# Second attention: the bias table in three bf16 parts on two column halves, and the reached matrices made by VectorE

## The chip, the cores and the metric

The kernel runs on one core of one Trainium2 chip. The time is the device time of one execution in microseconds (us); 3 runs of the kernel before are given, and their median is the reference. Less is better.

## The reference, cut to what matters

The reference is two transformer blocks over 256 tokens of width 1024, in float32. The second block holds, beside a state space branch, a sparse attention, and only this one is touched. For each of 256 queries and 16 heads the logits over 256 keys are a product with a latent of 128 numbers, plus a bias that depends on the distance between key and query, plus a mask that leaves the 64 best keys:

```python
bias = rel_bias[t5_bucket_2(pos_sel - pos_b[..., None])]       # 32 buckets, 16 heads
logits = jnp.einsum('bqhc,bqkc->bhqk', q_b, kv_sel).astype(jnp.float32) * scale
logits = logits + jnp.transpose(bias, (0, 3, 1, 2)).astype(jnp.float32)
logits = jnp.where(valid[:, None], logits, -jnp.inf)
probs = jax.nn.softmax(logits, axis=-1).astype(kv_sel.dtype)
return jnp.einsum('bhqk,bqkc->bqhc', probs, kv_sel)
```

## The kernel before

Weights stream through a ring of four 128x1024 tiles. Each is split into a high part (ScalarE, line 826, written as fp32r) and a low part (VectorE at line 1229, or GpSimd at line 655), and TensorE multiplies three combinations of high and low parts; in most stages that is line 1772 (`fm_tile`, six matmuls for one row block k: two column blocks of 128 with three products each). Every engine runs its own list of instructions in the order in which they are written, and semaphores join them.

The second attention is worked off in 32 tiles of 8 queries x 16 heads = 128 rows (`NTILE`, `QT`). For tile n TensorE adds up in one PSUM bank `lg` of 128 rows x 256 keys:

- the product of queries and latent, `uq` and `kvT`, in fp32 (line 2192, one matmul that the trace shows as two instructions),
- the bias: the jumps of the bias from bucket to bucket are in a table, one row for each bucket border; `reached[c]` has a 1 where a key lies past the border. The 128 contraction rows are 32 borders x 4 queries, so the 8 queries of a tile take two such matrices, c = 0 and 1. The table of c is zero in the 64 columns of the other four queries. It exists as a high and a low fp32r part, `tab_hi` and `tab_lo`, so that line 2196 is four matmuls of 128 columns of weights and 256 moving columns,
- the mask, one bf16 matmul (line 2197, in the trace's numbering).

Then follow, in the same list, for older tiles: two transposes of the probabilities of tile n-2 (line 2205), for even n one step of `fm_tile` of another product (`s_z2`, line 1772) as filler, and the product of probabilities and values of tile n-3 (line 2216). Behind the 32 tiles stands the head-wise output product (line 2223).

GpSimd makes `reached` (line 760): two `tensor_scalar` for each tile, into two buffers; for tile n it waits until TensorE is through with the logits of tile n-2. TensorE waits for it with `reach_ready`.

VectorE does for tile n: the row maximum (line 1604, behind the logits of n), the reciprocal and the scaling of the probabilities of n-1 (lines 1609 and 1610), the copy of the output of n-4 (line 1615), and at n = 0, 8, 16, 24 the low parts of the filler's weights (`split_to`, line 1229). ScalarE does the exponential (line 1123) and the copy of the transposed probabilities (line 1130), and the high parts at the same n.

The table is made about 55 us earlier: VectorE multiplies it out into `tab_f` (line 1558, fp32), ScalarE makes `tab_hi` (line 1097), and VectorE the rest `tab_lo` behind the few instructions that prepare the step sizes of the state space branch (lines 1564 to 1569). Next on VectorE comes the sum of the index scores (lines 1580 and 1582).

Of the kernel before, what the change touches and what calls it, by code (L numbers as in the profile page):

```python
# [21 lines left out]
F32 = mybir.dt.float32  # L22
F32R = mybir.dt.float32r
BF16 = mybir.dt.bfloat16
I32 = mybir.dt.int32
ALU = mybir.AluOpType
ACT = mybir.ActivationFunctionType
AX = mybir.AxisListType

P = 128  # L30
S = 256
# [21 lines left out]
H2, CKV = 16, 128  # L53
# [3 lines left out]
QT = 8  # L57
NTILE = S // QT
# [57 lines left out]
def _emit(nc, ctx, a, out):  # L116
    def sem(name):
        return ctx.enter_context(nc.semaphore(name))

    def sb(name, shape, dt=F32, where=ctx):  # L120
        return where.enter_context(nc.sbuf_tensor(name, shape, dt))

    bank = [ctx.enter_context(nc.psum_tensor(f"bank{i}", [P, 512], F32)) for i in range(8)]
# [8 lines left out]
    sb("before_pick", [P, 2, S], F32, before_pick)  # L133
    pick = sb("pick", [P, 16 * P], BF16, before_pick)
    before_pick.close()
    ff_hi = sb("ff_hi", [P, KF, S], F32R)
    ff_lo = sb("ff_lo", [P, KF, S], F32R)
    x_tok = sb("x_tok", [P, TT, D])
    work = sb("work", [P, KD, S])
# [107 lines left out]
    kin = oT_flat[:, 1024:1280].rearrange("p (t a d) -> p t a d", t=TT, a=2)  # L247
    junk = oT_flat[:, 1280:1280 + 6 * QR].rearrange("p (n k) -> p n k", n=6)

    reached = ff_hi[:, 16:20, :].rearrange("p (b c) s -> p b c s", b=2)  # L250
    tab_hi, tab_lo = (ff_lo[:, 16 + i, :].rearrange("p (c m) -> p c m", c=2) for i in range(2))
    work_flat = work[:, :, :].rearrange("p k s -> p (k s)")
    sums2 = work_flat[:, 0:512].unsqueeze(1)
    p2T = work_flat[:, 512:1024].rearrange("p (b k r) -> p b k r", b=2, k=2)
# [119 lines left out]
    def held_slot(u):  # L374
# [61 lines left out]
    reach_ready, lt_mm, lt_max, lt_exp, lt_p, lt_T, lt_pT, lt_pv, lt_o = (  # L436
        sem("reach_ready"), sem("lt_mm"), sem("lt_max"), sem("lt_exp"), sem("lt_p"), sem("lt_T"),
        sem("lt_pT"), sem("lt_pv"), sem("lt_o"))
    step_mm, tab_own, tab_split = sem("step_mm"), sem("tab_own"), sem("tab_split")
    uv_mm, uv_hi, uv_lo = sem("uv_mm"), sem("uv_hi"), sem("uv_lo")  # L440

    dt_a, dt_b, dt_ready, xbc_ready = (
# [158 lines left out]
    def _(pool):  # L601
# [150 lines left out]
        pool.wait_ge(ix_sum, 8)  # L752
        pool.dma_start(w_uv[:, :, :], a["w_uv_2"].rearrange("h c d -> c h d")).then_inc(uv_in, 16)

        pool.wait_ge(tab_ready, 1)
        for n in range(NTILE):
            if n >= 2:
                pool.wait_ge(lt_mm, n - 1)
            for c in range(2):
                ins = pool.tensor_scalar(reached[:, n % 2, c, :], pos_f[:, 0:S],  # L760
                                         own_pos[:, 2 * n + c:2 * n + c + 1], None, ALU.is_ge)
            ins.then_inc(reach_ready, 1)
        pool.wait_ge(uv_mm, 4)
        for j in range(4):
            load_ada(8, j)
# [37 lines left out]
    def _(act):  # L803
# [233 lines left out]
        for n in range(len(TILES1) + 2):  # L1037
# [10 lines left out]
            if n >= 2:  # L1048
                m = n - 2
# [42 lines left out]
        for b in range(s_qi.n):  # L1092
            before_block(s_qi, b)
            act.activation(qi[:, 2 * b:2 * b + 2, :], bank3[(s_qi.b0 + b) % 2], ACT.Copy
                           ).then_inc(act_read, 1)
        act.wait_ge(tab_own, 1)
        act.activation(tab_hi, tab_f_cm, ACT.Copy).then_inc(tab_split, 1)

        for r in range(8):
            act.wait_ge(ix_mm, r + 1)  # L1100
# [118 lines left out]
    def _(dve):  # L1219
# [8 lines left out]
        def lo_of(dst, src, hi):  # L1228
            return dve.tensor_tensor(dst, src, hi.bitcast(F32), ALU.subtract)  # L1229
# [319 lines left out]
        for k in range(2):  # L1549
# [5 lines left out]
        lo_of(ff_lo[:, 0:2, :], rn[:, :, :], ff_hi[:, 0:2, :]).then_inc(qn_lo, 1)  # L1555
        split_to(s_qi.u0 + 4)
        dve.wait_ge(step_mm, 1)
        dve.tensor_tensor(tab_f[:, :, :], bank[6][:, 0:H2].unsqueeze(1).broadcast_to([P, 2 * QT, H2]),
                          own_query.unsqueeze(2).broadcast_to([P, 2 * QT, H2]), ALU.mult).then_inc(tab_own, 1)

        dve.wait_ge(few_T, 2)
        dve.wait_ge(ssd_in, 48)
# [4 lines left out]
        link(dve.scalar_tensor_tensor(dt_sc[:, 1, :, :], dt_sc[:, 0, :, :], -1.0, dt_sc[:, 0, :, :],  # L1567
                                      ALU.mult, ALU.max))
        dve.tensor_scalar(dt_sc[:, 0, :, :], dt_sc[:, 0, :, :], 0.0, None, ALU.max).then_inc(dt_a, 1)
        dve.wait_ge(tab_split, 1)  # L1570
        lo_of(tab_lo, tab_f_cm, tab_hi).then_inc(tab_ready, 1)

        for r in range(8):
            qt, r4 = r // 4, r % 4
# [21 lines left out]
        dve.tensor_tensor(mask[:, :, :], isc[:, :, :], shut[:, :, :], ALU.add).then_inc(mask_ready, 1)  # L1596
        split_to(s_z2.u0)

        for n in range(NTILE + 4):
            if n < NTILE:  # L1600
                dve.wait_ge(lt_mm, n + 1)
                if n >= 4:
                    dve.wait_ge(lt_exp, n - 3)
                dve.tensor_reduce(st3[:, n % 4, 0:1], bank[2 + n % 2][:, 0:S], AX.X, ALU.max, negate=True
                                  ).then_inc(lt_max, 1)
            if 1 <= n <= NTILE:
                m = n - 1
                dve.wait_ge(lt_exp, m + 1)
                link(dve.reciprocal(st3[:, m % 4, 2:3], st3[:, m % 4, 1:2]))
                dve.tensor_scalar(p2buf[m % 4], p2buf[m % 4], st3[:, m % 4, 2:3], None, ALU.mult  # L1610
                                  ).then_inc(lt_p, 1)
            if n >= 4:
                m = n - 4
                dve.wait_ge(lt_pv, m + 1)
                dve.tensor_copy(oT[:, :, QT * m:QT * m + QT],
                                bank[6 + m % 2][:, 0:P].rearrange("p (q h) -> p h q", q=QT)
                                ).then_inc(lt_o, 1)
            if n % 8 == 0 and n < NTILE:
                split_to(s_z2.u0 + n // 8 + 1 + AHEAD)
        for b in range(4):  # L1620
# [108 lines left out]
    def _(pe):  # L1729
# [456 lines left out]
        for n in range(NTILE + 3):  # L2186
            if n < NTILE:
                lg = bank[2 + n % 2][:, 0:S]
                pe.wait_ge(reach_ready, n + 1)
                if n >= 2:  # L2190
                    pe.wait_ge(lt_exp, n - 1)
                pe.matmul(lg, uq[:, QT * n:QT * n + QT, :].rearrange("p q h -> p (q h)"), kvT[:, :],  # L2192
                          start=True, stop=False)
                for c in range(2):
                    for tab in (tab_hi, tab_lo):
                        pe.matmul(lg, tab[:, c, :], reached[:, n % 2, c, :], start=False, stop=False)  # L2196
                pe.matmul(lg, pick[:, (n % 16) * P:(n % 16 + 1) * P], mask[:, n // 16, :],
                          start=False, stop=True).then_inc(lt_mm, 1)
            if 2 <= n <= NTILE + 1:
# [116 lines left out]
```

## Time and profile before

| | |
|---|---|
| median of 3 runs | 1096.64 us (1095.22 to 1097.78) |
| the profiled execution, its own time | 1097.29 us |
| its span, first to last instruction | 1095.6 us |
| mean granted TensorE clock | 0.976 of full speed |
| TensorE matmuls busy | 1028.5 us, 94% |
| VectorE, ScalarE, GpSimd busy | 63%, 50%, 27% |
| the second attention's 32 tiles | from 494.55 to 568.03 us, 73.5 us |

A row of a timeline gives start, length, engine, line, operation, output and inputs, shapes, and in brackets the idle time before it with what ended it. "PE" is a matmul, "PEld" its weight load. A shape "128\*64" means 128 contraction rows and 64 columns of weights. Lengths of consecutive matmuls overlap (they are pipelined), so that what one costs is read from start to start, or from the chain, which has no overlap in it.

### The profile page before, as it was taken

Reading aid. Unit: us, or ns where it says so; the run is one execution under the profiler, and the core shown is the slowest. Engines: PE = TensorE matmul, PEld = TensorE weight load, DVE = VectorE, ACT = ScalarE, POOL = GpSimd, SP = SyncE. Lnnn points to the kernel's source line nnn. Section 1 sums busy time; section 2 is a strip of 40 time slices with the busy share of each in tenths; the row PEclk is TensorE's granted clock in tenths of the full one; section 3 lists DMA queues with packets and bytes.
Section 4 is the critical chain, followed back from the end, with each engine's and each line's share of the span. In section 5 each row is a group of like instructions: output and inputs, shape, how many; then the busy total and the mean of one; then the engine's idle time right before and its main releaser. Section 6 shows DMA issues by size and latency. Waiting matters only on the chain.

```text
span 1095.6 us, 17088 instructions
## 1 busy us (share of the span) xinstructions
PE 1028.5 (94%) x6328; PEld 894.9 (82%) x6328; DVE 691.7 (63%) x1166; ACT 547.2 (50%) x972; POOL 296.4 (27%) x274
## 2 busy tenths in 40 slices
PE   7998999899999987998999889989999989999998
PEld 6987777788887776798989889977799878888886
DVE  3476663778779564885556466665588566555553
ACT  4365455645443472834455566554464365444443
POOL 3010102411114253588951034334531240000000
PEclk9999799999999998999999989989999999999999
DMA  7577003788989731462119456640068564666562
GB/s 221 175 207 256 11 2 99 237 248 266 287 270 331 231 95 54 140 185 71 34 35 319 128 152 175 173 116 1 1 217 245 175 201 145 201 182 180 166 219 88
DMA packets 141359, 179.14 MB, mean 164 GB/s; under 512 B 7811, under 2 KB 117149, under 8 KB 141282
## 3 DMA queue, kind: packets, MB, share of 16 engines
q1 hardware_dynamic: 130624, 144.53, 42.8%
q0 software_dynamic: 10080, 33.19, 10.2%
q8 instruction: 47, 0.77, 0.3%
q10 hardware_dynamic: 578, 0.41, 0.1%
q14 instruction: 30, 0.25, 0.1%
HBM read 176.98 MB, written 1.11 MB: 163 GB/s over the span
## 4 chain that ended last, share of the span: by engine, by line
PE 80%; DVE 8%; ACT 6%; DMA 3%; issue 2%; POOL 1%; ACTq 0%; DVEq 0%; SPq 0%; POOLq 0%
PE bank L1772 24%; PE bank L1861 11%; PE bank L1863 11%; PE bank L1862 11%; PE bank L2263 2%; PE bank L2284 2%; PE bank L1957 1%; ACT w_hi L826 1%; DVE w_lo L1229 1%; DMA w_raw<-in_w_in 1%; PE bank L2104 1%; PE bank L2061 1%; DVE isc L1582 1%; PE bank L2196 1%; PE bank L2192 1%
## 5 line engine op out<-in xcount | busy, mean ns | idle before, releaser
L1229 DVE TENSOR_TENSOR w_lo<-w_raw,w_hi 128x1024 fp32r<-128x1024 f32 (+1 forms) x231 | 276.2, 1220 | 117.3 <-ACT w_hi L826 104.5
L826 ACT ACTIVATE w_hi<-w_raw 128x1024 fp32r<-128x1024 f32 (+1 forms) x258 | 261.0, 1036 | 146.5 <-PE bank L1863 58.3
L1772 PE MATMUL bank<-h_hi,w_hi 128*128 128x256 f32 x592 | 173.8, 294 | 11.2 <-DVE w_lo L1229 8.6
L1772 PE MATMUL bank<-h_lo,w_hi 128*128 128x256 f32 x592 | 170.2, 288 | 0.0
L1772 PE MATMUL bank<-h_hi,w_lo 128*128 128x256 f32 x592 | 170.1, 287 | 0.0
L1861 PE MATMUL bank<-w_hi,h_hi 128*128 128x512 f32 x384 | 151.5, 394 | 2.2 <-DVE h_lo L1229 2.2
L1863 PE MATMUL bank<-w_hi,h_lo 128*128 128x512 f32 x384 | 149.7, 390 | 0.0
L1862 PE MATMUL bank<-w_lo,h_hi 128*128 128x512 f32 x384 | 149.5, 389 | 0.0
L1772 PEld LDWEIGHTS bank<-h_hi,w_hi 128*128 128x128 f32 x592 | 116.4, 197 | 14.9 <-DVE w_lo L1229 9.4
L1772 PEld LDWEIGHTS bank<-h_lo,w_hi 128*128 128x128 f32 x592 | 116.5, 197 | 0.0
L1772 PEld LDWEIGHTS bank<-h_hi,w_lo 128*128 128x128 f32 x592 | 116.3, 196 | 0.0
L655 POOL TENSOR_TENSOR w_lo<-w_raw,w_hi 128x1024 fp32r<-128x1024 f32 (+1 forms) x35 | 76.2, 2177 | 127.7 <-DVE w_lo L1229 86.3
L1861 PEld LDWEIGHTS bank<-w_hi,h_hi 128*128 128x128 f32 x384 | 72.1, 188 | 16.8 <-issue 2.5
L1863 PEld LDWEIGHTS bank<-w_hi,h_lo 128*128 128x128 f32 x384 | 72.1, 188 | 15.2
L1862 PEld LDWEIGHTS bank<-w_lo,h_hi 128*128 128x128 f32 x384 | 72.2, 188 | 14.4
L681 POOL DMA_DIRECT2D ada_raw<-in_ada_w x48 | 35.1, 732 | 171.5 <-DVE ada_acc L1358 150.8
L1861 PE MATMUL bank<-w_hi,ff_hi 128*128 128x512 f32 x176 | 69.9, 397 | 3.3 <-DVE w_lo L1229 3.1
L1772 PE MATMUL bank<-ff_hi,w_hi 128*128 128x256 f32 x240 | 69.2, 288 | 3.0 <-DVE w_lo L1229 1.4
L1863 PE MATMUL bank<-w_hi,ff_lo 128*128 128x512 f32 x176 | 69.3, 393 | 0.0
L1862 PE MATMUL bank<-w_lo,ff_hi 128*128 128x512 f32 x176 | 69.1, 393 | 0.0
L1772 PE MATMUL bank<-ff_lo,w_hi 128*128 128x256 f32 x240 | 67.9, 283 | 0.0
L1772 PE MATMUL bank<-ff_hi,w_lo 128*128 128x256 f32 x240 | 67.8, 283 | 0.0
(432 smaller groups left out, 1987.1 us busy)
## 6 DMA issues: line engine op xcount, KB each, us to landing
w_raw<-in_w_in SPq DMA_DIRECT2D x84, 512.0 KB, 3.8
ada_raw<-in_ada_w POOLq DMA_DIRECT2D x48, 512.0 KB, 5.8
w_raw<-in_w_gate_up SPq DMA_DIRECT2D x88, 256.0 KB, 5.3
w_raw<-in_w_ffn_in SPq DMA_DIRECT2D x88, 256.0 KB, 3.4
w_raw<-in_w_down SPq DMA_DIRECT2D x22, 512.0 KB, 6.9
w_raw<-in_w_ffn_out SPq DMA_DIRECT2D x22, 512.0 KB, 4.4
w_raw<-in_w_out SPq DMA_DIRECT2D x16, 512.0 KB, 4.8
w_raw<-in_w_o_ssd SPq DMA_DIRECT2D x16, 512.0 KB, 5.1
```

Of the source, the lines that this page charges most:

```text
L655: pool.tensor_tensor(low(u, n), w_raw[:, u % RING, 0:n], high(u, n).bitcast(F32), ALU.subtract).then_inc(lo_ready, 1)
L681: pool.dma_start(ada_raw[:, j, :].rearrange("p (k c) -> p k c", k=2), ada[:, 2 * j:2 * j + 2, 512 * c:512 * c + 512]).then_inc(ada_in[j], 16)
L826: act.activation(high(u, n), w_raw[:, u % RING, 0:n], ACT.Copy).then_inc(hi_ready, 1)
L1229: return dve.tensor_tensor(dst, src, hi.bitcast(F32), ALU.subtract)
L1582: ins = dve.scalar_tensor_tensor(isc[:, qt, :], relu_s[:, r % 2, j, :], w, isc[:, qt, :], ALU.mult, ALU.add)
L1772: ins = pe.matmul(out_b[:, s, :], w[:, kk, c], x[:, k0 + k, :], start=k == 0 and s == 0 and step == 0, stop=k == sum(st.ks) - 1 and s == 1 ...
L1861: pe.matmul(out, x_hi[:, k + kk, x], hi, start=start and kk == 0, stop=False, skip_group_check=True)
L1862: pe.matmul(out, x_hi[:, k + kk, x], lo, start=False, stop=False, skip_group_check=True)
L1863: ins = pe.matmul(out, x_lo[:, k + kk, x], hi, start=False, stop=stop and kk == 1, skip_group_check=True)
L1957: pe.matmul(bank[b][:, 0:S], ones, mats[:, 0:S], start=True, stop=True)
L2263: pe.matmul(sg[:, 0:S], ud[:, h % 2, 0, :], tri_ones, start=True, stop=False, skip_group_check=True)
L2284: pe.matmul(bank[4 + i % 2][r64, 0:S], x_dt[:, 0, 64 * m:64 * m + 64], m_buf[:, m % 2, 0:S], start=True, stop=False)
```

## The change

- The table becomes three bf16 parts, `tabs[:, part, c, :]`, all made by VectorE directly behind `tab_f`: copy to bf16, subtract from `tab_f`, copy, subtract, copy. ScalarE's `tab_hi` and the wait for it go.
- `reached` becomes bf16, with three buffers instead of two, and is made by VectorE: those of tiles 0 and 1 ahead of the loop, that of tile n+2 in turn n, behind the output copy and ahead of `split_to`. GpSimd does nothing for the attention's loop any more.
- On TensorE the bias takes six bf16 matmuls instead of four fp32r ones. Each has only the 64 columns of weights that are not zero, and writes only 64 of the 128 partitions of `lg`: 0 to 63 for c = 0, 64 to 127 for c = 1, alternately.
- `tabs` and `reached` get buffers of their own at places in memory that lie over `ff_hi` and `ff_lo`, about where they were.

```diff
-        pool.wait_ge(tab_ready, 1)
-        for n in range(NTILE):
-            if n >= 2:
-                pool.wait_ge(lt_mm, n - 1)
-            for c in range(2):
-                ins = pool.tensor_scalar(reached[:, n % 2, c, :], pos_f[:, 0:S],
-                                         own_pos[:, 2 * n + c:2 * n + c + 1], None, ALU.is_ge)
-            ins.then_inc(reach_ready, 1)
         pool.wait_ge(uv_mm, 4)
...
-        act.wait_ge(tab_own, 1)
-        act.activation(tab_hi, tab_f_cm, ACT.Copy).then_inc(tab_split, 1)
...
-        dve.tensor_tensor(tab_f[:, :, :], bank[6][:, 0:H2].unsqueeze(1).broadcast_to([P, 2 * QT, H2]),
-                          own_query.unsqueeze(2).broadcast_to([P, 2 * QT, H2]), ALU.mult).then_inc(tab_own, 1)
+        ins = dve.tensor_tensor(tab_f[:, :, :], bank[6][:, 0:H2].unsqueeze(1).broadcast_to([P, 2 * QT, H2]),
+                          own_query.unsqueeze(2).broadcast_to([P, 2 * QT, H2]), ALU.mult)
+        for part in range(3):
+            link(ins)
+            ins = dve.tensor_copy(tabs[:, part, :, :], tab_f_cm)
+            if part < 2:
+                link(ins)
+                ins = dve.tensor_tensor(tab_f_cm, tab_f_cm, tabs[:, part, :, :], ALU.subtract)
+        ins.then_inc(tab_ready, 1)
...
-        dve.wait_ge(tab_split, 1)
-        lo_of(tab_lo, tab_f_cm, tab_hi).then_inc(tab_ready, 1)
...
+        def reach(n):
+
+            for c in range(2):
+                ins = dve.tensor_scalar(reached[:, n % 3, c, :], pos_f[:, 0:S],
+                                        own_pos[:, 2 * n + c:2 * n + c + 1], None, ALU.is_ge)
+            ins.then_inc(reach_ready, 1)
+
+        reach(0)
+        reach(1)
         for n in range(NTILE + 4):
...
+            if n + 2 < NTILE:
+                reach(n + 2)
             if n % 8 == 0 and n < NTILE:
                 split_to(s_z2.u0 + n // 8 + 1 + AHEAD)
...
-                for c in range(2):
-                    for tab in (tab_hi, tab_lo):
-                        pe.matmul(lg, tab[:, c, :], reached[:, n % 2, c, :], start=False, stop=False)
+                for part in range(3):
+                    for c in range(2):
+                        r64 = slice(64 * c, 64 * c + 64)
+                        pe.matmul(lg[r64, :], tabs[:, part, c, r64], reached[:, n % 3, c, :], start=False, stop=False,
+                                  skip_group_check=True)
```

## Rows read from the trace of the kernel before

**Rows 1.** Stages: PE, PEld, DVE, ACT, POOL busy (x), clock, DMA share, GB/s.

```profile
510.00:568.00 58.00, 55.96 (x429) 52.17 (x427) 32.82 (x113) 26.39 (x86) 48.73 (x49) 1.00 0.11 29
```

**Rows 2.** The chain that ended last, tiles 8 to 13: start, us, what.

```profile
513.52 0.43 PE bank L2192 x2
...
518.00 0.42 DVE st L1604
...
520.67 0.43 PE bank L2192 x2
521.11 0.47 PE bank L2196 x4
521.71 0.22 PE bank L2205 x2
...
522.37 0.43 PE bank L2192 x2
...
523.62 0.71 PE bank L1772 x6
...
524.78 0.43 PE bank L2192 x2
```

**Rows 3.** Lines 760, 1609, 1610, 1615: duration ns min/median/max, first and last start.

```profile
L760 POOL TENSOR_SCALAR ff_hi<-pos_f,own_pos x64: 913/923/2492, 489.9 to 561.1; 128x256 fp32r<-128x256 f32 x64
L1609 DVE RECIPROCAL st<-st x32: 150/154/164, 501.4 to 565.2; 128x1 f32<-128x1 f32 x32
L1610 DVE TENSOR_SCALAR isc<-isc,st x16: 354/380/480, 505.1 to 565.4; 128x256 f32<-128x256 f32 x16
L1615 DVE COPY oT<-bank x32: 272/283/292, 507.3 to 567.6; 128x128 f32<-128x128 f32 x32
```

**Rows 4.** Timeline: matmuls of alternating column halves with nothing else between them.

```profile
102.11 2.02 PE L2072 MATMUL bank<-wsT,gv 128*64 128x128 f32 x32
568.03 3.67 PE L2223 MATMUL bank<-oT,work 128*64 128x256 f32 x32 [0.47 <-DVE oT L1615]
```

**Rows 5.** Timeline of the state space stage: one turn between full and half width.

```profile
739.60 0.70 PE L2263 MATMUL bank<-mats,work 128*128 128x256 f32 x2
740.14 0.38 PE L2265 MATMUL bank<-mats,dtd 128*128 128x128 f32 x2
740.36 0.39 PE L2267 MATMUL bank<-mats,work 128*128 128x128 f32 x2
740.68 0.65 PE L2284 MATMUL bank<-work,x_dt 128*64 128x256 f32 x2
741.16 0.38 PE L2286 MATMUL bank<-work,x_dt 128*64 128x128 f32 x2
741.47 0.70 PE L2263 MATMUL bank<-mats,work 128*128 128x256 f32 x2
```

**Rows 6.** Groups from 500 to 564 us, weight loads: count, busy us, mean ns.

```profile
L2196 PEld LDWEIGHTS bank<-ff_hi,ff_lo 128*128 128x128 f32 x123 | 19.3, 193 | 1.6
...
L2197 PEld LDWEIGHTS bank<-mask,pick 128*128 128x128 bf16 x31 | 3.0, 97 | 1.4
```

**Rows 7.** Groups of VectorE from 494 to 568 us: busy, mean ns, idle before.

```profile
L1229 DVE TENSOR_TENSOR w_lo<-w_raw,w_hi 128x1024 fp32r<-128x1024 f32 x6 | 7.4, 1261 | 3.4 <-ACT w_hi L826 3.4
```

**Rows 8.** Waits from 494 to 570 us: total us, times, longest.

```profile
DVE st L1604 <- PE bank L2197: 30.5, 25, 6.0
```

**Rows 9.** Timeline of the first tiles of the attention.

```profile
497.52 0.58 PE L1772 MATMUL bank<-h_hi,w_hi 128*128 128x256 f32 x1 [1.70 <-DVE w_lo L1229]
...
503.24 0.30 PEld L2192 LDWEIGHTS bank<-kvT,uq 128*128 128x128 f32 x2 [0.34 <-POOL ff_hi L760]
```

**Rows 10.** Timeline of VectorE where the table is made.

```profile
436.25 0.42 DVE L1558 TENSOR_TENSOR tab_f<-bank,mats 128x256 f32<-128x256 f32 x1
...
439.75 0.43 DVE L1229 TENSOR_TENSOR ff_lo<-tab_f,ff_lo 128x256 fp32r<-128x256 f32 x1 [1.00 <-ACT ff_lo L1097]
441.80 0.35 DVE L1580 TENSOR_SCALAR isc<-work,widx 128x256 f32<-128x256 f32 x1 [1.63 <-ACT work L1104]
```

More of the change, by code:

```diff
@@ L135, in _emit @@
     before_pick.close()
+    before_reached = ExitStack()
+    sb("before_reached", [P, 16, S], F32, before_reached)
+    reached = sb("reached", [P, 3, 2, S], BF16, before_reached)
+    before_reached.close()
     ff_hi = sb("ff_hi", [P, KF, S], F32R)
+    before_tabs = ExitStack()
+    sb("before_tabs", [P, 16, S], F32, before_tabs)
+    tabs = sb("tabs", [P, 3, 2, QT * H2], BF16, before_tabs)
+    before_tabs.close()
     ff_lo = sb("ff_lo", [P, KF, S], F32R)
@@ L248, in _emit @@
     junk = oT_flat[:, 1280:1280 + 6 * QR].rearrange("p (n k) -> p n k", n=6)
-    reached = ff_hi[:, 16:20, :].rearrange("p (b c) s -> p b c s", b=2)
-    tab_hi, tab_lo = (ff_lo[:, 16 + i, :].rearrange("p (c m) -> p c m", c=2) for i in range(2))
     work_flat = work[:, :, :].rearrange("p k s -> p (k s)")
@@ L438, in _emit @@
         sem("lt_pT"), sem("lt_pv"), sem("lt_o"))
-    step_mm, tab_own, tab_split = sem("step_mm"), sem("tab_own"), sem("tab_split")
+    step_mm = sem("step_mm")
     uv_mm, uv_hi, uv_lo = sem("uv_mm"), sem("uv_hi"), sem("uv_lo")
```

## The prediction

> **What bounds the kernel now.** I read the page first: TensorE's matmuls are busy for 94% of the span, so the question is whether the 32 tiles of the second attention are part of that. Then the table of stages: from 510 to 568 us TensorE is busy 56.0 of 58.0 us at the full granted clock (1.00), GpSimd 48.7, VectorE 32.8, ScalarE 26.4 [rows 1]. Then the chain that ended last, which has no overlap in it: it runs on TensorE from tile to tile. A tile with no filler takes 522.37 - 520.67 = 1.70 us, the next one, with six filler matmuls (0.71), 2.41, a pair 4.11 [rows 2]. From the start of line 2192 to the transposes the bias takes 0.47 us, 0.118 for each of four matmuls [rows 2]. Sixteen pairs are 65.8 us of the 73.5 us that the stage lasts; the other 7.7 lie mostly in its first four tiles. A smaller part is in the three later splits of VectorE: tiles 8 to 10 take 520.67 - 513.52 = 7.15 us, 0.63 more than the 2.41 + 1.70 + 2.41 of a long, a short and a long tile, and there the chain leaves TensorE for the row maximum of tile 9, which stands behind the split on VectorE [rows 2].
>
> GpSimd is close behind: two `reached` at 0.92 to 0.94 us each are 1.9 us of an average tile's 2.05 [rows 3]. Close, but the chain shows it late only near the start (part 4). So taking this work off GpSimd is worth little by itself. What counts is what becomes of TensorE's 0.47 us.
>
> **Part 1, the six half-width matmuls.** The trace has nothing like them in bf16, but it has fp32 matmuls of alternating halves. 32 instructions of 128 moving columns take 2.02 us; without the tail of the last (0.27) that is 1.75/31 = 0.056 us each, and 32 of 256 columns 3.67, or (3.67 - 0.38)/31 = 0.106 [rows 4]. At full width the same kind costs 0.11 (two in 0.22) and 0.215 (two in 0.43) [rows 2]. So the two halves run at the same time, and 0.056 us is a pace at which a load and a matmul can be issued. A one-pass matmul of 256 columns costs 0.118 at full width, so half of it, 0.056 to 0.059, is what I take for each of the six: 0.34 us. Bounds: 0.32 (three pairs at the array's 0.107, half of fp32's 0.215), and 0.71 if bf16 halves do not overlap (6 x 0.118).
>
> The Trainium skill, page "TensorE: Matmul & The Clock Gate", section on packing small matmuls, says that weight loads overlap running matmuls only where the row group differs; both halves here use all 128 rows. By that each of the six would pay for itself, the 0.71 above. The rows of alternating halves speak against it: they share all rows too, and go at half price.
>
> **Part 2, getting into half width and out again.** This is the term that the diff does not show. In the state space stage each head does three products at full width and two at half width. Start to start: 0.54, 0.22, 0.32, 0.48, 0.31, together 1.87 us [rows 5]. The same five at the prices of a run without a change of width (fp32 of 256 columns 0.44, of 128 columns 0.22 [rows 2]) are 0.44 + 0.22 + 0.22 + 0.44 + 0.22 = 1.54. The difference, 0.33 us, is the price of going in and out once. The surplus sits exactly at the changes: 0.10 in front of and 0.04 behind the way in, 0.09 and 0.10 at the way out.
>
> The Trainium skill, page "TensorEngine Tiling (Array Packing)", section Key Properties, says that a change of tiling mode drains TensorE. The rows agree, with 0.33 us for two changes.
>
 So up to 0.09 us is saved: 0.24 to 0.33, and I take 0.28. The far bounds are 0 (the load finds cover) and 0.35.
>
> Bias per tile: 0.34 + 0.28 = 0.62 against 0.47, **+0.15 us**, times 32 = **+4.8 us**. TensorE is the chain here, so all of it counts.
>
> **Part 3, VectorE in the loop.** It gets two more instructions in each tile. The nearest row is line 1610, same engine, same operation with a scalar per row, 128x256, fp32 out: 0.35 to 0.48, median 0.38 [rows 3]. Two are 0.76, at worst 0.96; bf16 output could make them a little dearer or cheaper, and GpSimd's silence a little cheaper. VectorE's present work for a tile is 0.42 for the row maximum [rows 2] and 0.154 + 0.38 + 0.283 for the rest [rows 3], 1.24 us, so 2.0 then, at worst 2.2, against TensorE's 2.05 + 0.15 = 2.20. Starts overlap ends by 0.05 to 0.1 us each, so it is really nearer 1.75. In the short tiles (1.85 us) VectorE may fall behind by a tenth; the long ones (2.56) let it catch up, and the transposes of n-2 need only what VectorE did one turn before. Nothing on the chain, then.
>
> At a split `reach` stands in front of it, but there VectorE waits for ScalarE's high part, 3.4 us at the three later splits, 1.1 each [rows 7], which is cover for 0.7. The 0.63 us lost at each of three splits is a delay fixed by ScalarE and VectorE, seen against TensorE's next two tiles. These get 2 x 0.15 longer, so the loss falls by 0.3 each: **-0.9 us**.
>
> **Part 4, the first tiles.** `reach(0)` and `reach(1)` fall in the 6.0 us in which VectorE waits for the first logits [rows 8]: nothing. In turn 0 `reach(2)` goes ahead of three splits, and TensorE already waits 1.7 us for the first of them [rows 9]: +0.7. At 503.24 the weight load of tile 3 waits 0.34 us for GpSimd [rows 9]; that goes, with a little more at tile 4: -0.5. **+0.2 us.**
>
> **Part 5, making the table.** Behind `tab_f` at 436.25 come three copies and two subtractions, 3 x 0.36 + 2 x 0.43 with 0.05 between, 2.2 us; the old subtraction (0.43) and the 1.0 us of waiting ahead of it go. The index scores start at 441.80, when ScalarE's output is there, and VectorE had 1.63 us of idle time in front of that [rows 10]. 2.2 - 0.43 - 1.0 = 0.8 fits into 1.63. Cost nothing; without the cover it would be up to 0.8 us, as the index scores are on the chain next. ScalarE's `tab_hi` (0.41) goes where ScalarE then waits for TensorE: nothing.
>
> **Sum:** 4.8 - 0.9 + 0.2 = +4.1 us. On the profiled execution's own 1097.29 us (span 1095.6 and 1.7 around it) that is 1101.4; that execution lies 0.65 above the median, so for the median 1096.64 + 4.1 = **1100.7 us**. Behind the attention TensorE goes on being the chain, so nothing gives it back.
>
> **Rivals.**
> A, *the drain is covered*: bf16 loads are short, the queue hides them, and a change costs 0.05 or less instead of 0.14. For: the exposed loads are half as long [rows 6]. Against: in the state space stage the matmuls show the gap, not just the loads [rows 5]. Free changes give 0.34 against 0.47, 32 x -0.13 = -4.2; the stalls at the splits grow by 3 x 0.26 = +0.8, start +0.2: **1093.4 us**. It turns from slower to faster where both changes together cost less than 0.13 us.
> B, *halves do not overlap in bf16*: 0.71 + 0.28 - 0.47 = +0.52 a tile, 16.6 us, minus 1.9 for the stalls, which then vanish: **1111.5 us**. The rows of halves speak against it.
> C, *VectorE becomes the bound*: if the two instructions cost 0.5 each and nothing overlaps, 8 tiles and a split are 8 x 2.24 + 1.26 = 19.2 us against TensorE's 17.6, that is +1.6 for 8 tiles: **about 1107 us**. Against it: VectorE's idle share of 43% [rows 1] and the overlapping starts.
> D, *in between*: the changes cost about 0.1 us for both or a little more, and the sum ends within 2 us of nothing: **1096.6 us**.
>
> **How the numbers follow.** Forecast (changes 0.20 to 0.35 us a tile, 1098.9 to 1103.5) 0.52; A 0.22; D 0.14; B 0.07; C 0.05. A measurement of this kernel tells about 0.2% (2.2 us) from no change. Slower by more: forecast, B and C, with a little of the forecast's low edge given away, 0.61; within: D and that edge, 0.17; faster: A, 0.22. The range reaches from A's 1093 to beyond the forecast's upper end and to C's edge, 1106; B and the far part of C, about 1 in 10, are left out with a little of A.
>
> **What the profile will show.** Right: no GpSimd work in the stage; on TensorE a gap of about 0.1 us between line 2192 and the first half matmul and one behind the last, six starts 0.056 apart; a pair of tiles in 4.4 us; VectorE busy some 55 of 73 us with TensorE still the chain. Wrong: six starts 0.11 apart (B); no gap (A); row maximum or line 1610 on the chain in most tiles (C); pairs in under 4.1 us.

## The result, and the profile after

The changed kernel takes 1103.68 us (1102.1 to 1106.95, 4 runs) against 1096.6 us of the kernel before beside it (1095.22 to 1097.78, 4 runs): 1.0075 times as long, 95% interval 1.0056 to 1.0094. In a second, longer measurement it was 1.0042 [1.0029, 1.0055]. The profiled execution has a span of 1105.2 us, 1106.95 in all, and a mean granted clock of 0.972.

| | before | after |
|---|---|---|
| median | 1096.6 us | 1103.7 us |
| the 32 tiles | 73.4 us | 75.9 us |
| VectorE busy, 510 to 568 us | 32.8 of 58 [rows 1] | 45.0 of 58 |
| GpSimd busy, 510 to 568 us | 48.7 of 58 [rows 1] | 0 |
| GpSimd busy in all | 27% | 21% |

The same stretch of the changed kernel (TensorE, its weight loads, VectorE, ScalarE, GpSimd busy; clock; DMA share; GB/s):

```profile
510.00:568.00 58.00, 57.55 (x486) 42.89 (x486) 44.99 (x163) 25.98 (x85) 0.00 (x0) 1.00 0.11 29
```

The chain that ended last, changed kernel: one long tile, the start and end of the short one behind it, and the stall behind the split at tile 8. Line 2204 is the product of queries and latent, 2209 the six halves, 2211 the mask, 2219 the transposes, 1784 the filler, 2230 the values:

```profile
513.05 0.43 PE bank L2204 x2
513.48 0.45 PE bank L2209 x6
513.93 0.21 PE bank L2211
514.15 0.22 PE bank L2219 x2
514.37 0.71 PE bank L1784 x6
515.08 0.45 PE bank L2230 x4
515.53 0.43 PE bank L2204 x2
...
517.29 0.43 PE bank L2204 x2
...
518.42 0.43 DVE st L1614
...
522.36 0.36 DVE work L1620
...
522.77 0.44 PE bank L2219 x2
...
524.37 0.43 PE bank L2204 x2
```

A pair takes 517.29 - 513.05 = 4.24 us where it took 4.11 [rows 2]. The bias is 0.45 instead of 0.47, so nothing is lost there; the loss is in the mask behind it, 0.215 instead of 0.13. Its matmul is the same as before; it now stands behind a change of width. From 517.29 to 524.37 are 7.08 us for a long, a short and a long tile of 2.48 + 1.76 + 2.48 = 6.72, so a split costs 0.36 us instead of 0.63.

Tile 4 in the timeline of the changed kernel shows both gaps at the weight loads:

```profile
509.17 0.25 PEld L2209 LDWEIGHTS bank<-reached,tabs 128*64 128x64 bf16 x6 [0.33 <-issue]
509.18 0.52 PE L2209 MATMUL bank<-reached,tabs 128*64 128x256 bf16 x6
509.62 0.10 PEld L2211 LDWEIGHTS bank<-mask,pick 128*128 128x128 bf16 x1 [0.20 <-issue]
```

VectorE's new work, from the list of groups and from the timeline of the first tiles (changed kernel):

```profile
L1603 DVE TENSOR_SCALAR reached<-pos_f,own_pos 128x256 bf16<-128x256 f32 x64 | 19.4, 346 | 0.0
```

```profile
498.44 0.61 DVE L1603 TENSOR_SCALAR reached<-pos_f,own_pos 128x256 bf16<-128x256 f32 x2
498.96 3.49 DVE L1225 TENSOR_TENSOR w_lo<-w_raw,w_hi 128x1024 fp32r<-128x1024 f32 x3
...
500.23 0.58 PE L1784 MATMUL bank<-h_hi,w_hi 128*128 128x256 f32 x1 [2.17 <-DVE w_lo L1225]
```

346 ns each where I had 380. Two are 0.61 in a row, and between the first split and the last tile VectorE is on the chain only at the splits.

And the table, VectorE, changed kernel:

```profile
438.89 0.29 DVE L1558 CAST tabs<-tab_f 128x256 bf16<-128x256 f32 x1
439.22 0.42 DVE L1561 TENSOR_TENSOR tab_f<-tab_f,tabs 128x256 f32<-128x256 f32 x1
439.68 1.28 DVE L1558 CAST tabs<-tab_f 128x256 bf16<-128x256 f32 x1
440.99 1.50 DVE L1561 TENSOR_TENSOR tab_f<-tab_f,tabs 128x256 f32<-128x256 f32 x1
442.53 0.29 DVE L1558 CAST tabs<-tab_f 128x256 bf16<-128x256 f32 x1
...
443.99 0.35 DVE L1581 TENSOR_SCALAR isc<-work,widx 128x256 f32<-128x256 f32 x1 [0.18 <-ACT work L1100]
```

It took 3.9 us instead of 2.2: two of the five instructions took 1.3 and 1.5 us, and GpSimd was at work nearly all that time (two `tensor_tensor`, 2.89 us from 439.32 us on). The idle time ahead of the index scores went from 1.63 [rows 10] to 0.18 us: covered, by a hair.

**Where the rest is.** The tiles explain 2.4 of 7 us. So I cut every profile at the same instructions: the first logits, the first product behind the tiles (uv), the first and the last product of the state space stage, and the last product of the gated mixing ahead of the second feed-forward (called the turn below). In us:

| kernel | before tiles | tiles | uv to state space | state space | to the turn | rest |
|---|---|---|---|---|---|---|
| before | 494.6 | 73.4 | 156.8 | 70.5 | 114.5 | 185.8 |
| before, again | 490.7 | 73.3 | 157.2 | 70.6 | 114.4 | 185.7 |
| after | 496.7 | 75.9 | 157.5 | 70.7 | **118.7** | 185.7 |
| after, again | 493.6 | 75.8 | 157.4 | 70.6 | **118.8** | 185.8 |

The first column differs by 3.9 and 3.1 us between two executions of the same kernel. The third and fourth together are 0.9 us more after than before in the first pair, 0.2 in the second. The fifth is the surprise: 4.3 us, in a stretch that begins 230 us behind the edit and has no changed instruction in it.

### The profile page after: what moved, and what is told of

It reads as the page before. It is cut to its first block, busy times and chain, and to the rows that moved or that the text cites. A ratio compares the mean times of both kernels' runs of the same rounds, so it can differ in the third digit from the quotient of the medians.

```text
span 1105.2 us, 17219 instructions
## 1 busy us (share of the span) xinstructions
PE 1036.2 (94%) x6392; PEld 887.2 (80%) x6392; DVE 709.1 (64%) x1234; ACT 547.3 (50%) x971; POOL 233.7 (21%) x210
## 3 DMA queue, kind: packets, MB, share of 16 engines
q0 software_dynamic: 10080, 33.19, 10.2%
## 4 chain that ended last, share of the span: by engine, by line
PE 80%; DVE 8%; ACT 6%; DMA 3%; issue 2%; POOL 1%; ACTq 0%; DVEq 0%; SPq 0%; POOLq 0%
PE bank L1784 24%; PE bank L1873 11%; PE bank L1875 11%; PE bank L1874 11%; PE bank L2277 2%; PE bank L2298 2%; DMA w_raw<-in_w_in 2%; PE bank L1969 1%; ACT w_hi L824 1%; DVE w_lo L1225 1%; PE bank L2116 1%; PE bank L2073 1%; PE bank L2204 1%; PE bank L2209 1%; DVE isc L1583 1%
```

## The experiments

**The same kernels again, and each half of the change alone.** `before_again` and `after_again` are the two kernels unchanged.

> The kernel before, unchanged, as a yardstick: ratio to itself 1.000 within 0.002, about 1096.6 us. What matters is the second profile of it. If the 7 us between the two kernels come with the change, this profile agrees with the first one stage by stage to a few tenths (attention loop 73.5 us, start of the loop at 494.5). If the stretches outside the attention that wait for loads (the first 10 us, 804 to 816, 870 to 910) move by themselves, this profile differs from the first one there by 1 us or more, with an equal attention loop.

> The changed kernel, unchanged. Theory 'all in the loop': the loop costs 75.8 us again, 2.4 more than before, the rest of the 7 us was scatter, and five rounds give a ratio of 1.002 to 1.004. Rival 'something behind the loop': the ratio stays at 1.006 to 1.009 (about 1103.5 us), the loop is again only 2.4 us longer, and the profile shows 3 to 5 us lost in the same stretches behind 724 us as the first profile.

`te_alone` keeps the table and the six halves, and gives `reached` back to GpSimd, in two buffers:

```diff
+        for n in range(NTILE):
+            if n >= 2:
+                pool.wait_ge(lt_mm, n - 1)
+            for c in range(2):
+                ins = pool.tensor_scalar(reached[:, n % 2, c, :], pos_f[:, 0:S], ...)
...
-                reach(n + 2)
```

> The table in three bf16 parts and the six half-width matmuls as in the changed kernel, but GpSimd makes the reached matrices (bf16, two buffers, the old waits). Theory 'TensorE's matmuls cost it': pairs of tiles in 4.24 us as in the changed kernel, loop +2 us, whole kernel +2 to +3 us (1099 us) if nothing else matters. Rival 'moving the reached matrices costs it': the kernel is within 1 us of before plus the 2 us of the loop, while the run with VectorE alone shows 3 to 5 us. GpSimd needs 1.9 us of a tile's 2.12, so it does not bound.

`dve_alone` is the kernel before with only `reached` moved to VectorE, in three fp32r buffers:

```diff
-            for c in range(2):
-                ins = pool.tensor_scalar(reached[:, n % 2, c, :], pos_f[:, 0:S], ...)
...
+            if n + 2 < NTILE:
+                reach(n + 2)
```

> The kernel before with fp32r table and four full-width matmuls; only the reached matrices (fp32r, three buffers) are made by VectorE, at the places of the changed kernel. Theory 'TensorE's matmuls cost it': pairs stay at 4.11 us, start +0.2 us, kernel within 0.5 us of before (1096.8). Rival 'moving the work costs it': 1099 to 1102 us, with the loss outside the pairs. Rival 'VectorE becomes the bound': row maximum on the chain in most tiles, pairs over 4.3 us.

| kernel | ratio to before | tiles | to the turn |
|---|---|---|---|
| before_again | 0.9992 [0.9978, 1.0006] | 73.3 | 114.4 |
| after_again | 1.0042 [1.0029, 1.0055] | 75.8 | 118.8 |
| te_alone | 1.0035 [1.0021, 1.0049] | 74.9 | 117.5 |
| dve_alone | 0.9998 [0.9983, 1.0014] | 73.9 | 114.4 |

For `after_again` both theories were half right: the ratio fell as the first one had it (1.0042), but the profile shows the 4.4 us behind the state space stage that the rival had named. `te_alone` costs 3.8 us by its ratio where 2 to 3 were expected, 1.6 of them in the tiles. Moving `reached` alone is worth nothing in the total. The loss belongs to the edit on TensorE, and more of it lies in the stretch to the turn (3.1 to 4.4 us) than in the tiles (1.6 to 2.5). In both kernels with the late loss the records of the queue that brings TensorE's code ("q8 instruction": 47 packets and 0.77 MB in 1105 us, some 16 KB each) differ in one respect: counted from the last product of the state space stage, the packets come at about 4, 34, 48, 64 and 84 us in `before` and `dve_alone`, and at about 0, 14, 42 to 44, 58 and 74 to 76 us in `after` and `te_alone`. The 64 more matmuls with their loads make TensorE's code 8 KB longer, half a packet. (That size is worked out from packets: `after_pad` below has 256 instructions more than `before` and 48 packets instead of 47, `twelve_halves` has 512 more and 49 packets, so 128 instructions are half a packet.) From 10 to 22 us behind that product the weight loads fill all 16 DMA engines (a share of 1.00 in `before`, 1.01 in `after`), and the chain runs over one of them.

**Only the length of the code.** Both kernels got 128 instructions at the head of TensorE's list that count up a semaphore of their own, 8 KB of code:

```diff
+        for _ in range(128):
+            pe.sem_inc(pad_sem, 1)
```

> The kernel before with the same 128 counting instructions at the head of TensorE's list: 8 KB more code, as much as the change adds. Nothing is left out. Theory (code packets): a packet at about +14 us behind the last state space product, that stretch 117.5 to 118.8 us instead of 114.4, tiles 73.4, ratio 1.003 to 1.004. Rival (the loss belongs to the change's arithmetic): 114.4 stays and the ratio is 1.000.

> The changed kernel, with 128 instructions that only count up a semaphore nobody waits for, put at the head of TensorE's list. They lengthen TensorE's code by 8 KB more, 16 KB in all against the kernel before, which is one whole packet of the queue that brings in the code. Nothing is left out. Theory (the 3 to 4.4 us lost behind the state space stage come from a code packet that lands in the stretch in which weight loads fill all DMA engines): the packets fall again at +4, +34, +48 us and so on behind the last state space product, none at +14; from there to the turn of the second feed-forward 114.4 to 115 us instead of 118.7; the attention's 32 tiles unchanged at 75.8; total 3.5 to 4 us below the changed kernel, ratio to the kernel before 1.000 to 1.003. Rival (that loss belongs to the arithmetic of the change, for example to the granted clock after a denser stretch, and the packets only go along with it): 118.7 stays, ratio 1.004 to 1.008.

I had priced the 128 instructions at nothing. They cost 12 to 13 us: TensorE's first matmul starts at 20.4 us, and at 7.2 to 8.6 in six kernels without them, so the totals (1113.04 and 1112.81 us, ratios 1.0156 [1.0134, 1.0178] and 1.0151 [1.0128, 1.0175]) don't answer the question directly, and the ratio expected for either was missed. The stages do:

| kernel | code against before | packets behind the state space stage | tiles | to the turn |
|---|---|---|---|---|
| before | 0 | 4, 34, 48 us | 73.4 | 114.5 |
| before_pad | +8 KB | 14, 44, 60 us | 73.4 | **118.7** |
| after | +8 KB | 0, 14, 44 us | 75.9 | **118.7** |
| after_pad | +16 KB | 4, 32, 48 us | 75.7 | 115.6 |

The late loss goes with the length of the code, not with the arithmetic. `before_pad` computes exactly what `before` computes. And with both padded the two totals are level: the tiles' +2.3 us stand against -3.1 to the turn.

How it looks in the trace. Chain of waits, `before_pad`, at the product ahead of the gate:

```profile
816.92 11.90 DMA w_raw<-in_w_in
```

and the same place in the kernel before:

```profile
805.64 10.72 DMA w_raw<-in_w_in
...
816.39 1.07 ACT w_hi L826
...
817.48 0.98 DVE w_lo L1229
```

The DMA view of 4 us, from 12 to 16 us behind the last state space product, `before_pad` (packets, MB, share of 16 engines):

```profile
...
q8 instruction: 1, 0.02, 1.8%
```

In `before` the same 4 us have no q8 line. 1.8% of 16 engines over 4 us is 1.15 us of one engine, and the load on the chain is 1.18 us longer. TensorE's stall behind it grows from 1.45 to 1.83 us (a further one of 0.53 us lies 5 us ahead of it), and then the granted clock drops. Stretches of 4 us at the stall and at the next one, 50 us later (columns as above), `before_pad`:

```profile
834.60:838.60 4.00, 2.41 (x11) 2.44 (x12) 4.00 (x4) 2.35 (x3) 2.04 (x2) 0.71 0.51 116
838.60:842.60 4.00, 4.00 (x32) 4.00 (x31) 3.96 (x6) 1.07 (x1) 0.75 (x1) 0.87 0.85 288
...
886.60:890.60 4.00, 3.23 (x8) 2.59 (x9) 4.00 (x7) 2.52 (x3) 1.09 (x2) 0.61 0.49 188
```

and the same three in `before`:

```profile
823.30:827.30 4.00, 3.57 (x30) 3.60 (x31) 4.00 (x4) 1.51 (x2) 1.39 (x2) 1.00 0.80 220
827.30:831.30 4.00, 4.00 (x35) 3.93 (x34) 3.96 (x6) 2.04 (x2) 0.75 (x1) 1.00 0.81 227
...
875.30:879.30 4.00, 4.00 (x19) 3.30 (x18) 3.38 (x3) 1.10 (x2) 0.00 (x0) 1.00 0.97 328
```

0.71, 0.87 and 0.61 are mixtures of the two levels, 2.4 and 1.2 GHz; `before` holds 2.4 in all three. Set side by side matmul by matmul, `after_again` is 1.4 us behind `before_again` when the stall ends (0.8 of it from the new stall 5 us ahead, 0.6 from this one), loses 1.5 us more in the slow stretch behind it, and 1.5 at the second stall: 4.4 in all.

The longer stall is not always followed by a low clock. `te_alone` has both stalls (0.75 and 1.83 us) and loses 1.4 us by them, and then:

```profile
827.20:831.20 4.00, 2.22 (x18) 2.25 (x19) 4.00 (x4) 2.68 (x4) 2.04 (x2) 1.00 0.50 112
831.20:835.20 4.00, 4.00 (x35) 3.94 (x34) 3.96 (x6) 1.06 (x1) 0.74 (x1) 1.00 0.84 291
```

Its clock drops at the second stall alone, which is why it reaches the turn in 117.5 us and not in 118.7. What makes the clock drop at the second stall I can't say: TensorE idles there for 2.2 us in kernels whose clock drops and in kernels whose clock doesn't. `after_pad` has a drop there too (0.71 and 0.87), which is its 1.1 us above `before`.

So the packet's place is worth 1.4 us by itself here, and the rest of the 4.4 us is the clock. How often that comes can be read from the mean granted clock of every execution. In `after_again` it is 0.971 for the profiled one, which is also the slowest of the six, and 0.976 or 0.977 for the other five (in the first measurement 0.972, and 0.973 to 0.976 for the others); the kernel before beside it has 0.974 to 0.981, mean 0.9774. The two drops take about 0.003 off a mean ((0.29 + 0.13 + 0.39) x 4 us and a little more, of 1102). An estimate from these: most executions of `after_again` had less low clock than the profiled one, and so the 6.6 us that the stages add up to are more than the usual loss, 4.6 by the second measurement.

**Two parts of the table.** `two_parts` has the shape of the change and the code length of the kernel before:

```diff
-                for part in range(3):
+                for part in range(2):
```

> The changed kernel with two bf16 parts of the table instead of three: four half-width matmuls for each tile. It leaves out the third part of the table, so the bias is rounded to about 16 bits. TensorE's code is as long as before. Theory (halves 0.056 us each, two changes of width 0.22 us for both): a pair of tiles 4.24 - 2 x 0.112 = 4.02 us, the 32 tiles 75.8 - 3.6 plus up to 0.7 given back at the splits = 72.3 to 73; behind the state space stage 114.4 to 115 (code packets where they were); total 1 us below the kernel before to 0.5 above, ratio 0.998 to 1.001. Rival 1 (the loss behind the state space stage is not the code's): 118.7 there, ratio 1.002 to 1.004. Rival 2 (the three parts cost by the change of partition, not of width, 0.12 for each part): a pair 4.24 - 2 x 0.22 = 3.8, tiles 69.

0.9995 [0.9977, 1.0013]; tiles 73.0, to the turn 114.4, the packets at 4, 32, 48, 64 and 84 us. All three as the theory of the code's length had it. Chain:

```profile
508.23 0.43 PE bank L2204 x2
508.67 0.34 PE bank L2209 x4
509.01 0.21 PE bank L2211
```

Two halves fewer take 0.34 instead of 0.45: 0.055 us each. This says what was wrong with the change itself: the third part is 0.11 us a tile, and without it the edit breaks even, with a bias that is rounded to about 16 bits.

**Six at full width.** `full_six` has the same six matmuls with all 128 columns, the table's zeros among them, and so no change of width:

```diff
-                        pe.matmul(lg[r64, :], tabs[:, part, c, r64], reached[:, n % 3, c, :], ...)
+                        pe.matmul(lg, tabs[:, part, c, :], reached[:, n % 3, c, :], start=False, stop=False)
```

> The changed kernel with the six bf16 matmuls at full width (128 columns of weights, the table's zeros included), so no change of width and the same arithmetic. Code as long as that of the changed kernel. Theory (halves overlap, a change of width costs about 0.11 us each): six at 0.107 to 0.118 make 0.64 to 0.71 in the chain against 0.45 for the halves with their way in, and the mask 0.11 against 0.215, so +0.09 to 0.15 us a tile, a pair 4.42 to 4.54, tiles 78.5 to 80.5 us, total 3 to 5 us above the changed kernel, ratio 1.008 to 1.011. Rival (bf16 halves gain nothing by themselves and a change of width costs nothing): the tiles stay at 75.8, ratio 1.004 to 1.006.

1.0086 [1.0063, 1.0109], tiles 78.5, to the turn 118.6 (a packet at 14 us again). Chain, line 2208 the six, 2209 the mask:

```profile
508.48 0.65 PE bank L2208 x6
509.13 0.11 PE bank L2209
```

A full-width bf16 matmul costs 0.109 us and the mask, with no change of width before it, 0.11. So halves do go at half price, and the way out costs 0.215 - 0.11 = 0.105.

**Twelve halves, and another order.** `twelve_halves` issues the six twice, `c_major` swaps the two loops:

```diff
-                for part in range(3):
+                for part in (0, 1, 2, 0, 1, 2):
```

```diff
-                for part in range(3):
-                    for c in range(2):
+                for c in range(2):
+                    for part in range(3):
```

> The changed kernel with the six half-width matmuls issued twice in a row; the bias is then added twice, so the computation is changed by that. No further change of width is added. Theory (halves overlap in pairs, 0.056 us each): line 2209 takes 0.45 + 6 x 0.056 = 0.78 us in the chain, the mask still 0.215, a pair 4.24 + 0.67 = 4.91 us, and the 32 tiles 75.8 + 10 = 86 us. Rival (the six cost 0.45 because each costs 0.075 and the way in nothing): 0.90 us, a pair 5.14, tiles 90.

> The changed kernel with the order of the six halves turned: three parts for partitions 0 to 63 one after the other, then three for 64 to 127. Same arithmetic. Theory (two halves run side by side only where they alternate): the three of one half cost about 0.11 us each, six 0.6 us or more with the way in instead of 0.45, +0.15 to 0.3 us a tile, tiles 80 to 85 us. Rival (the pace is that of issuing a 64-column load and a matmul, whatever half they go to): 0.45 us as before, tiles 75.8.

`twelve_halves`, chain:

```profile
506.89 0.78 PE bank L2209 x12
507.67 0.21 PE bank L2211
```

`c_major`, chain:

```profile
506.65 0.46 PE bank L2209 x6
507.10 0.22 PE bank L2211
```

Six more halves are 0.33 us, 0.055 each, so the way in is 0.45 - 0.33 = 0.12, exactly as expected; the tiles take 85.1 us (the splits then cost nothing: eight tiles in 19.57 us, and 4 x (2.09 + 2.80) = 19.56). It has 256 matmuls and 256 loads more than `before`, 32 KB or two whole packets of code (24 KB beyond `after`), so by the packets it belongs with `before`: they come at 4, 32 and 48 us again, and its stretch to the turn takes 114.3 us. The total, from a single timing (1108 us), is the lengthened tiles alone. `c_major` ran against what I had expected: three halves of the same side in a row cost no more than alternating ones, and its tiles take 75.8 us (its one timing is 1106 us, with 118.8 to the turn).

**Room for the load.** `after_loads` and `two_parts_loads` move two of four 512 KB modulation loads of GpSimd out of the way of that weight load:

```diff
-        for j in range(4):
+        for j in range(2):
             load_ada(10, j)
         for b in range(s_gb.n):
...
+            if b < 2:
+                load_ada(10, b + 2)
```

> The changed kernel, with two of the four modulation loads that GpSimd issues behind the state space stage (each 512 KB) moved behind the two gating products that follow them on its list, 3 and 8 us later. VectorE needs them only 10 us and more behind that. TensorE's code and its packets stay where they are in the changed kernel, nothing is left out. Theory (the packet at +14 us costs because it makes the last transfer of w_raw<-in_w_in late in a stretch in which the transfers are the limit): with 1 MB less ahead of it that transfer lands in 8 to 10.5 us instead of 12.0, the stall of TensorE in front of the attention's gate products shrinks from 1.83 us, and the stretch to the turn of the second feed-forward takes 112.5 to 115 us instead of 118.7, although a packet still falls at +14; ratio to the kernel before 0.999 to 1.002. Rival 1 (TensorE itself waits for its instructions when the packet comes there, whatever the weights do): 117 to 118.7, ratio 1.003 to 1.005. Rival 2 (later modulation data hold up VectorE): slower than the changed kernel, VectorE waiting for ada_raw.

> The kernel with two parts of the table (its third part left out, as in two_parts) and the same two loads moved back. Theory: in the kernel before, too, the chain runs over that transfer (10.7 us) before TensorE's stall of 1.35 us, so the stretch falls from 114.4 to 112 to 113.8 us, and with tiles at 73.0 us the total is 1 to 3 us below the kernel before, ratio 0.997 to 0.999. Rival (the stall is set by VectorE's order of splits and modulation behind the transfer): 114.4 stays and the ratio is 0.9995.

| kernel | ratio | the stretch's two loads w_raw<-in_w_in, median landing | to the turn |
|---|---|---|---|
| after | 1.0075, again 1.0042 | 10.2 us | 118.7 |
| after_loads | 1.0053 [1.0033, 1.0073] | 7.1 us | 117.8 |
| two_parts | 0.9995 [0.9977, 1.0013] | 9.0 us | 114.4 |
| two_parts_loads | 0.9992 [0.9970, 1.0015] | 6.2 us | 115.5 |

Both expectations were missed. The transfers that I took for the cause land 3 us sooner, and only 0.9 us comes back: the stall of 0.59 us ahead of the long one is gone, and the long one is 1.97 us instead of 1.84. The chain goes over the next transfer now, `after_loads`:

```profile
815.03 10.09 DMA w_raw<-in_w_o_ssd
```

and over the same one of 9.36 us in `two_parts_loads`, where no packet comes. So the packet's 0.7 us are found on whichever load is last in a stretch in which the DMA engines, not one transfer, are the limit. In `after_loads` the clock drops at both stalls as before. On two parts of the table the stretch gets 1.1 us longer, and that isn't the loads: up to the second stall `two_parts_loads` is 0.2 us ahead of `two_parts`, and there its clock drops where that of `two_parts` stayed at 1.00:

```profile
868.70:872.70 4.00, 2.22 (x5) 1.82 (x6) 3.97 (x7) 2.53 (x3) 1.09 (x2) 0.70 0.27 80
```

That the packet's place decides is shown (`before_pad`, `after_pad`, and `two_parts` and `twelve_halves` fit it); that it does so by way of this one load is not, and the part that comes back by making room is small.

## Why the prediction came out as it did

The forecast was 1100.7, in a range of 1093 to 1106; the first measurement is 1103.7, the second puts the change at +4.6 us by its ratio, near the forecast's +4.1. The side and the range were right, the reasons only in part, and the near agreement is partly luck: the tiles lost 2.4 us and not the 4.1 forecast, and a stretch that the prediction left out lost 4.3 in the profiled executions.

- **Part 1, 0.056 us for each half**: right in price, 0.055 (`twelve_halves`, `two_parts`). Rival B is out. The sign that I had named, six starts 0.056 apart, did not come: the timeline records the starts in pairs, with 0.11 to 0.13 us from pair to pair. Its explanation is not settled. I read the rows of alternating halves [rows 4] as two halves side by side; `c_major` shows that they need not alternate. Its first pair is two halves for the same partitions 0 to 63 (from narrow windows; the first numbers are the starts of the three pairs, xN counts what is merged into a row):

```profile
506.58 0.31 PE L2209 MATMUL bank<-reached,tabs 128*64 128x256 bf16 x2
506.71 0.39 PE L2209 MATMUL bank<-reached,tabs 128*64 128x256 bf16 x4
506.82 0.28 PE L2209 MATMUL bank<-reached,tabs 128*64 128x256 bf16 x2
```

  Either the sides work off what is queued for them in any order, or a half-width matmul is that quick by itself. Halves of one side only would tell; that wasn't tried. The Trainium skill, page "TensorEngine Tiling (Array Packing)", Key Properties, says that different tiles can load and multiply in parallel; the price agrees with it, and no run here proves it.
- **Part 2, the changes of width**: right in kind, too dear by a quarter: 0.12 in and 0.105 out, 0.22 for both, where I took 0.28 from 0.24 to 0.33. The value lies just under the lower bound. The rows of fp32 [rows 5] held 0.33 with exposed fp32 loads on both sides; I took off the mask's shorter load (0.09) only in part, and the way in has a short load too. Bias and mask together went up by 0.065 us a tile, 2.1 us in all, not 4.8. **This is the term that was mis-sized.** It makes 0.055 of the 0.085 us between the forecast's 0.15 and 0.065; 0.01 are the halves (0.33, not 0.34), and 0.02 the mask, which takes 0.13 us in the kernel before and 0.11 behind bf16 matmuls at full width (`full_six`), and which the sum had left alone. Rival A (changes at 0.05 each or less) is out by the same numbers.
- **Part 3, VectorE**: never the bound, rival C is out: 346 ns for each of the new instructions. The stall of a split fell by 0.27 us, -0.8 in all, against my -0.9, and that is luck. The mechanism in the sum was right, two tiles' lengthening, but it gives only 2 x 0.065 = 0.13: in `te_alone`, which has the longer tiles and GpSimd at work, the stall is 0.50 us. `two_parts` and `full_six` follow it too, counted from `dve_alone`'s 0.49: tiles 0.05 us shorter and 0.16 longer than in the kernel before, stalls 0.58 and 0.17. The other 0.14 is what `dve_alone` gives, with tiles as they were: the scaling behind the split is on the chain, and it takes 0.36 us instead of 0.51 where GpSimd does nothing beside it. Two errors cancelled, the lengthening too large and this term at nothing. The chains of `before`, `te_alone` and `dve_alone`, in this order:

```profile
518.53 0.51 DVE work L1610
```

```profile
522.87 0.51 DVE work L1619
```

```profile
521.12 0.36 DVE work L1611
```

- **Part 4, the first tiles**: +1.1 us instead of +0.2. From tile 0 to tile 8 are 20.57 us against 18.97, of which 8 x 0.065 are the tiles' own. The wait for the first split grew by 0.5 (2.17 against 1.70 [rows 9]) where I had said 0.7, and the wait for GpSimd at tile 3 is gone. What I left out was the clock behind it: in the second 4 us of the stage the granted clock is 0.73 before and 0.50, the low level throughout, after. It comes with `reached` on VectorE: `dve_alone` and `two_parts` have the 0.50 too, `te_alone`, cut the same way, nothing below 0.73.

Changed kernel:

```profile
500.72:504.72 4.00, 4.00 (x19) 2.28 (x20) 2.54 (x6) 0.39 (x2) 0.00 (x0) 0.50 0.80 213
```

Kernel before:

```profile
498.55:502.55 4.00, 4.00 (x22) 3.50 (x22) 2.72 (x7) 0.60 (x3) 2.22 (x3) 0.73 0.95 257
```

  The 7.7 us beyond sixteen pairs do not lie mostly in the first four tiles, as the prediction reads them: the first eight tiles hold 2.5 of them (18.97 against 4 x 4.11), the three later splits 1.9, and 3.3 come behind the last tile. No term of the sum hangs on it.

- **Part 5, the table**: nothing, as said, though the work took 1.7 us longer than I reckoned and the cover was nearly used up.
- **"Behind the attention TensorE goes on being the chain, so nothing gives it back"**: this step failed. Nothing is given back, but 4.3 us more are taken, since 64 more matmuls are also 8 KB more code, and that put a packet of code among the weight loads that are on the chain 230 us later. The sum by parts: tiles 2.1 - 0.8 + 1.1 = +2.4, to the turn +4.2. The two profiled executions differ by 9.6 us; of the other 3.0, 2.1 lie ahead of the tiles, where the same kernel varies by 3 to 4 us, and 0.9 behind them, where two executions of the same kernel differ by 0.5 and 0.2. The medians differ by less, 7.1 and 4.6 us, and the clock of the executions that weren't profiled (above) says why in part.

For the change on its own merits, apart from where the code happens to lie, the tiles say +2.4 us, which is at the edge of what can be told from nothing. No version ran faster than the kernel before by more than its uncertainty; the two with two parts are level with it (0.9 us below by the ratio of `two_parts_loads`, with an interval from 3.3 below to 1.6 above).

## What to carry to other kernels

Price a change of column width as a step of its own (here 0.22 us there and back) and set it against what the halves save; a half in place of a full-width matmul saves 0.055, so it takes four of them to pay for one excursion, and two further ones cost 0.11 us again. When a time moves in a stretch that the edit doesn't touch, cut both traces at common instructions first; if the amount of code changed, pad the old kernel to the new length before looking for a mechanism. Pad where the engine waits anyway, or read the stage and not the total.

## What the runs showed of the hardware that was not expected

- TensorE's code comes in by packets of 16 KB over the same DMA engines as the weights. One of them took 1.8% of 16 engines over 4 us, and a 512 KB load on the chain went from 10.7 to 11.9 us.
- Behind a stall that had grown from 1.45 to 1.83 us the granted clock was 0.71 and 0.87 in the next two stretches of 4 us instead of 1.00, which cost 1.5 us more; in `te_alone` the same stall was followed by 1.00. In the case of the second stall, of 2.2 us in kernels of both kinds, the clock dropped only in some.
- 128 instructions that do nothing but count up a semaphore put off TensorE's first matmul from 7.2 to 8.6 us to 20.4 us, so they took at least 0.09 us each (TensorE had some idle time ahead of it before) and at most 0.16 (20.4 by 128).
- Half-width bf16 matmuls of 256 columns follow one another in 0.055 us even when they go to the same 64 partitions.
- VectorE's copy of 128x256 from fp32 to bf16 took 0.29 us alone and 1.28 with GpSimd at work beside it, the subtraction 0.42 and 1.50; the scaling behind a split took 0.51 with it and 0.36 without.
